# Last down projection of a two-layer decoder step: h as the stationary operand, 512 weight columns moving, the result by tokens

## The chip, the cores and the metric

The kernel runs on one core of one Trainium2 chip. The metric is the device time of one execution in microseconds (us), the median over runs. "The profiled execution" is one further execution, taken with the hardware profiler on; the views of the trace come from it alone.

## The reference, cut to what matters

There are 256 prompt tokens and 64 sample tokens (8 sequences of 8), D_MODEL is 2048, D_FF is 5632, and all is float32. The step has two layers; layer 0 mixes tokens by a convolution, layer 1 by an mLSTM cell, and each mixer is followed by a SwiGLU FFN. The change is in the FFN of layer 1, the last thing that is computed:

```python
x = x + rms_norm(mix, norm_mix_post[i])
f = swiglu_ffn(rms_norm(x, norm_ffn_pre[i]), ffn_w_gate[i], ffn_w_up[i], ffn_w_down[i])
xs[gi] = x + rms_norm(f, norm_ffn_post[i])        # y_prompt, y_sample after layer 1

def swiglu_ffn(x, w_gate, w_up, w_down):
    return _dense(jax.nn.silu(_dense(x, w_gate)) * _dense(x, w_up), w_down)

def rms_norm(x, g):                               # the mean is over the 2048 features of one token
    y = xf * lax.rsqrt(jnp.mean(xf * xf, axis=-1, keepdims=True) + RMS_EPS)
    return y * g
```

## The kernel before

**Layout.** Everything lies by features: `x`, `branch` and the rest are [128 partitions = features of a chunk, chunk, 320 tokens], with T = 320 = 256 prompt tokens and 64 sample tokens. The vectors of the norms are then columns (`vcol`), one value per partition, and a sum over the features of a token is a matmul with a matrix of ones.

**Phases, groups, units.** `plan` lays the dense products out as phases. A group is 512 output features; a unit is 256 contraction rows of weights by 512 columns (128 x 1024 floats in a slot of `raw`). The FFN of a layer is cut in two segments of D_FF: `up1a` (12 groups of 8 units), `down1a` (4 groups of 12 units), `up1b` (10 groups of 8), `down1b` (4 groups of 10). The down projection of layer 1 thus has 48 + 40 = 88 units.

**Three products for one.** Outside of `pw1`, weights and activations are split into a float32r part and the remainder (`hi` and `lo`, `hh` and `hl`), and a product is hi by hi, hi by lo, lo by hi (`unit`, L1415 to L1417). The weights are the stationary operand (128 x 128), the activations move, 320 columns at a time, and the result lands by features in a bank of PSUM. A unit of the down projection has 4 (128-feature pieces) x 2 (chunks of 128 rows) x 3 = 24 matmuls. A plain float32 matmul stands in the trace as two records, each with a weight load of its own (L1668 has 64 matmuls in the program and x128 in the trace); a float32r matmul stands there as one.

**Weights.** SP loads them unit by unit into 4 slots (`load`, L380). A load waits until `lo` of the unit four earlier was made (`lo_done`); ACT copies `raw` to `hi` when PE has used the slot's last unit (`units_used`, L561); DVE makes `lo` (L889); PE waits for `lo_done`. Both splits run AHEAD = 3 units before PE.

**Groups alternate between two halves of PSUM** (`bank_of`), four banks each. After a group of `down1a`, ACT copies the four banks to `branch` (`plain_out`); after a group of `down1b`, DVE adds them to it (`add_branch`, L912), ACT squares the sums (`squares`, L586) and DVE adds the squares up in `acc` (L904).

**The end.** After the last group: a matmul of `acc` with ones (`stat_post`, L1448), ACT's root (L567), DVE's `reciprocal` of all 320 columns (L923), then eight times branch times 1/rms (L1069) and twice x plus g times that (L1072), PE's transposes of `x` to token rows (L1744), ACT's copies to `y_rows` (L878), and SP's 12 stores (L408, L409).

```python
mm(out, hi[:, slot, kk, cols], rhs_hi[:, k, :], start=begin, stop=False, skip_group_check=True)
mm(out, hi[:, slot, kk, cols], rhs_lo[:, k, :], start=False, stop=False, skip_group_check=True)
ins = mm(out, lo[:, slot, kk, cols], rhs_hi[:, k, :], start=False, stop=end, skip_group_check=True)
```

**Other matmuls that the prediction refers to.** In the mLSTM cell, L1668 multiplies 64 stationary columns (`qw_seq[:, b, :]`) by 256 moving columns of `C0`, in plain float32, and writes alternately to partitions 0 to 63 and 64 to 127 of a bank: eight matmuls in a row. L1671 is a float32 matmul with 128 stationary columns right behind it, L1686 one of 32 rows, L1693 to L1696 are float32 matmuls on the full array.

Of the kernel before, what the change touches and what calls it, by code (L numbers as in the profile page):

```python
# [59 lines left out]
def trunk_kernel(  # L60
# [45 lines left out]
    with ctx:  # L106
# [25 lines left out]
        branch = sb("branch", [P, C, T])  # L132
        raw = sb("raw", [P, SLOTS, 2, 512])
# [7 lines left out]
        hh = sb("hh", [P, segs[0], T], F32R)  # L141
        hl = sb("hl", [P, segs[0], T], F32R)
        shared_end = at[0]
# [9 lines left out]
        root = sb("root", [P, T])  # L153
        sq = sb("sq", [P, 2, 2, T])
        acc = sb("acc", [P, T])
# [73 lines left out]
        here = [shared_at]  # L229
        y_rows = sb("y_rows", [P, 3, D], place=here)  # L230
# [19 lines left out]
        def vec(name, c, n=1):  # L250
# [39 lines left out]
        C_out, Cp_out, m_out, n_turned, n_copied, y_turned, y_copied, y_out, stored = (  # L290
            sem(n) for n in ("C_out", "Cp_out", "m_out", "n_turned", "n_copied", "y_turned", "y_copied", "y_out", "stored"))
# [30 lines left out]
        def tail_weights(j, slot):  # L322
# [5 lines left out]
            yield quads[:, :, P:2 * P], w[:, :, D + col:D + col + P]  # L328

# [40 lines left out]
        def _(sp):  # L370
# [33 lines left out]
            for k in range(C // 4):  # L404
                cols = slice(512 * k, 512 * (k + 1))
                sp.wait_ge(y_copied, 3 * (k + 1))
                for t in range(2):
                    sp.dma_start(y_prompt[0, t * P:(t + 1) * P, cols], y_rows[:, t, cols]).then_inc(y_out, 16)  # L408
                sp.dma_start(y_sample.rearrange("b t d -> (b t) d")[:, cols], y_rows[0:TS, 2, cols]).then_inc(y_out, 16)  # L409
            sp.wait_ge(y_out, 16 * 3 * (C // 4))  # L410
# [3 lines left out]
        def _(pool):  # L414
# [106 lines left out]
            pool.dma_start(n_prompt[0].rearrange("b h k -> (b h) k"), vrows[B * H:B * H + H, 0, :]).then_inc(stored, 16)  # L521
            pool.wait_ge(Cp_out, 16 * H)
# [30 lines left out]
        def _(act):  # L553
# [40 lines left out]

            def up_first_half(e):
# [3 lines left out]
            def up_second_half(e, chunk):  # L599
                act.wait_ge(up_prod, e + 1)  # L600
                s.activation(hh[:, bass.ds(chunk, 2), :], tB[:, :, :], ACT.Copy).then_inc(up_hi, 1)  # L601
# [1178 lines left out]
```

## Time and profile before

| | us |
|---|---|
| median of 3 runs | 3052.49 |
| the runs | 3052.45, 3055.36, 3052.49 |
| the profiled execution | 3051.82 |
| its span, first to last instruction | 3050.3 |
| TensorE busy | 2920.4 (96%) |
| VectorE busy | 1560.3 (51%) |
| ScalarE busy | 1074.5 (35%) |

The profiled execution took 1.52 us more than its span. Engines are PE (TensorE matmul), PEld (TensorE weight load), DVE (VectorE), ACT (ScalarE), POOL (GpSimd) and SP (SyncE, which issues the weight loads). Line numbers are those of the kernel before. Matmuls are pipelined: the length of a record is longer than the distance to the next one, so the pace of PE is read from starts.

### The profile page before, as it was taken

Reading aid. Unit: us, or ns where it says so; the run is one execution under the profiler, and the core shown is the slowest. Engines: PE = TensorE matmul, PEld = TensorE weight load, DVE = VectorE, ACT = ScalarE, POOL = GpSimd, SP = SyncE. Lnnn points to the kernel's source line nnn. Section 1 sums busy time; section 2 is a strip of 40 time slices with the busy share of each in tenths; the row PEclk is TensorE's granted clock in tenths of the full one; section 3 lists DMA queues with packets and bytes.
Section 4 is the critical chain, followed back from the end, with each engine's and each line's share of the span. In section 5 each row is a group of like instructions: output and inputs, shape, how many; then the busy total and the mean of one; then the engine's idle time right before and its main releaser. Section 6 shows DMA issues by size and latency. Waiting matters only on the chain.

```text
span 3050.3 us, 49093 instructions
## 1 busy us (share of the span) xinstructions
PE 2920.4 (96%) x18542; PEld 2765.6 (91%) x18542; DVE 1560.3 (51%) x2021; ACT 1074.5 (35%) x1267; POOL 78.6 (3%) x119
## 2 busy tenths in 40 slices
PE   8999598999999999998999999998999999999997
PEld 5777498999999999998788888998999999999997
DVE  1899946544433444445654544446544433444444
ACT  3223454433333333333333233344333333333333
POOL 2110000000000000000000000000000000000000
PEclk9999799999999999999999999999999999999999
DMA  6334143444444444444243535444444444444442
GB/s 176 125 124 124 49 147 119 150 147 151 149 148 151 150 147 151 148 150 138 76 144 116 161 108 164 136 148 127 146 151 148 148 152 148 148 151 148 148 152 90
DMA packets 374564, 423.30 MB, mean 139 GB/s; under 512 B 27034, under 2 KB 302210, under 8 KB 374114
## 3 DMA queue, kind: packets, MB, share of 16 engines
q1 hardware_dynamic: 367776, 399.61, 41.2%
q0 software_dynamic: 5744, 22.21, 2.4%
q8 instruction: 51, 0.84, 0.1%
q10 hardware_dynamic: 960, 0.38, 0.1%
q14 instruction: 33, 0.27, 0.0%
HBM read 409.22 MB, written 14.31 MB: 139 GB/s over the span
## 4 chain that ended last, share of the span: by engine, by line
PE 84%; DVE 12%; issue 2%; ACT 2%; DMA 0%; DVEq 0%; ACTq 0%; SPq 0%
PE PS L1415 26%; PE PS L1416 26%; PE PS L1417 26%; DVE branch L978 7%; PE PS L1413 1%; DVE lo L889 1%; DVE branch L1010 1%; DVE C L1346 1%; PE PS L1668 0%; PE PS L1661 0%; PE PS L1686 0%; ACT sq L679 0%; PE PS L1448 0%; PE PS L1621 0%; DVE branch L974 0%
## 5 line engine op out<-in xcount | busy, mean ns | idle before, releaser
L889 DVE TENSOR_TENSOR lo<-raw,hi 128x1024 fp32r<-128x1024 f32 x688 | 842.3, 1225 | 1140.9 <-ACT hi L561 1140.7
L1415 PE MATMUL PS<-xh,hi 128*128 128x320 f32 x4096 | 1283.9, 313 | 64.1 <-issue 34.0
L1416 PE MATMUL PS<-xl,hi 128*128 128x320 f32 x4096 | 1275.5, 311 | 0.0
L1417 PE MATMUL PS<-xh,lo 128*128 128x320 f32 x4096 | 1275.1, 311 | 0.0
L561 ACT ACTIVATE hi<-raw 128x1024 fp32r<-128x1024 f32 x688 | 724.7, 1057 | 1176.5 <-PE PS L1417 1176.5
L1415 PEld LDWEIGHTS PS<-xh,hi 128*128 128x128 f32 x4096 | 776.9, 190 | 81.4 <-issue 46.4
L1416 PEld LDWEIGHTS PS<-xl,hi 128*128 128x128 f32 x4096 | 777.3, 190 | 0.0
L1417 PEld LDWEIGHTS PS<-xh,lo 128*128 128x128 f32 x4096 | 776.3, 190 | 0.0
L1417 PE MATMUL PS<-hh,lo 128*128 128x320 f32 x1408 | 435.8, 310 | 0.0
L1416 PE MATMUL PS<-hl,hi 128*128 128x320 f32 x1408 | 435.8, 310 | 0.0
L1415 PE MATMUL PS<-hh,hi 128*128 128x320 f32 x1408 | 435.8, 310 | 0.0
L1416 PEld LDWEIGHTS PS<-hl,hi 128*128 128x128 f32 x1408 | 264.4, 188 | 0.0
L1415 PEld LDWEIGHTS PS<-hh,hi 128*128 128x128 f32 x1408 | 264.4, 188 | 0.0
L1417 PEld LDWEIGHTS PS<-hh,lo 128*128 128x128 f32 x1408 | 264.4, 188 | 0.0
L1413 PE MATMUL PS<-xg,raw 128*128 128x320 f32 x896 | 244.9, 436 | 0.0
L1413 PEld LDWEIGHTS PS<-xg,raw 128*128 128x128 f32 x896 | 171.1, 192 | 70.1 <-issue 1.4
L978 DVE SCALAR_TENSOR_TENSOR branch<-u_win,vcol,branch 128x320 f32<-128x320 f32 x420 | 206.4, 567 | 0.0
L597 ACT ACTIVATE tA<-tA 128x640 f32<-128x640 f32 x44 | 32.5, 739 | 99.2 <-DVE tA L930 99.2
L601 ACT ACTIVATE hh<-tB 128x640 f32 (+1 forms) x44 | 32.6, 741 | 90.5 <-DVE tB L937 90.5
L606 ACT ACTIVATE tB<-tB,vcol 128x320 f32<-128x320 f32 x14 | 7.1, 554 | 155.9 <-DVE tB L949 155.9
L619 ACT ACTIVATE u_win<-u_prm 128x1216 f32<-128x1216 f32 x16 | 38.8, 2427 | 17.4 <-DVE branch L978 6.5
L1322 DVE TENSOR_TENSOR tC<-root,PS 128x320 f32<-128x320 f32 x8 | 3.9, 488 | 78.9 <-ACT root L828 78.9
(277 smaller groups left out, 1310.6 us busy)
## 6 DMA issues: line engine op xcount, KB each, us to landing
raw<-in_ffn_w_gate SPq DMA_DIRECT2D x352, 256.0 KB, 2.8
raw<-in_ffn_w_up SPq DMA_DIRECT2D x352, 256.0 KB, 3.0
raw<-in_ffn_w_down SPq DMA_DIRECT2D x352, 256.0 KB, 3.3
raw<-in_conv_w_pw SPq DMA_DIRECT2D x192, 256.0 KB, 2.9
raw<-in_mlstm_w_v SPq DMA_DIRECT2D x64, 256.0 KB, 3.1
raw<-in_mlstm_w_out SPq DMA_DIRECT2D x64, 256.0 KB, 3.2
raw<-in_mlstm_w_q SPq DMA_DIRECT2D x64, 128.0 KB, 2.2
raw<-in_mlstm_w_k SPq DMA_DIRECT2D x64, 128.0 KB, 2.4
```

The source lines that it names most:

```text
L561: s.activation(hi[:, slot, :, :], raw[:, slot, :, :], ACT.Copy).then_inc(hi_done, 1)
L597: s.activation(tA[:, :, :], tA[:, :, :], ACT.Silu).then_inc(up_silu, 1)
L601: s.activation(hh[:, bass.ds(chunk, 2), :], tB[:, :, :], ACT.Copy).then_inc(up_hi, 1)
L619: s.activation(grid[:, :, 0:TP // L], past, ACT.Copy)
L889: v.tensor_tensor(lo[:, slot, :, :], raw[:, slot, :, :], hi[:, slot, :, :].bitcast(F32), ALU.subtract).then_inc(lo_done, 1)
L978: v.scalar_tensor_tensor(out=out, in0=u, scalar=w_j, in1=out, op0=ALU.mult, op1=ALU.add).then_inc(conv_step, 1)
L1010: v.scalar_tensor_tensor(out=out, in0=u, scalar=vec("w_dw", c + j * C), in1=out, op0=ALU.mult, op1=ALU.add).then_inc(tail_step, 1)
L1346: v.scalar_tensor_tensor(out=C0[:, b, :], in0=C0[:, b, :], scalar=g_state[:, b:b + 1], in1=PS[:, 5 + 2 * i, pair % 2 * DV:(pair % 2 + 1) * ...
L1413: ins = mm(out, raw[:, slot, kk, cols], xg[:, k, :], start=begin, stop=end, skip_group_check=True)
L1415: mm(out, hi[:, slot, kk, cols], rhs_hi[:, k, :], start=begin, stop=False, skip_group_check=True)
L1416: mm(out, hi[:, slot, kk, cols], rhs_lo[:, k, :], start=False, stop=False, skip_group_check=True)
L1417: ins = mm(out, lo[:, slot, kk, cols], rhs_hi[:, k, :], start=False, stop=end, skip_group_check=True)
```

## The change

For the last down projection (`down1a`, `down1b`) the operands change places. A new `unit_tok` takes the place of `unit`: the 128 tokens of a half of the prompt are the stationary operand (`hh`, `hl`), and 512 weight columns move (`hi`, `lo`), so that a unit has 2 (halves of the prompt) x 2 (chunks) x 3 = 12 float32r matmuls. The 64 sample tokens are kept in plain float32 (`h_smp`) and multiplied with the unsplit weights (`raw`), 256 columns at a time, once to partitions 0 to 63 and once to 64 to 127: 2 x 2 = 4 float32 matmuls a unit. The result lies by tokens (`b_rows`, `b_smp`). Since PE now reads `raw`, the loads of `down1a`, `up1b` and `down1b` wait for `units_used` and not for `lo_done`. POOL loads the post-norm's vector to all partitions (`g_rows`, `g_smp`) when `down1b` begins. DVE adds the group and multiplies by g at once (`tok_add`), ACT squares with a sum along the row (`tok_squares`); the norm is then one number per partition. At the end x is transposed into PSUM first and ten DVE instructions write y = y * inv + x^T, each followed by its store.

```diff
+            def unit_tok(p, g_bank, j, slot, quad, n, h_hi, h_lo):
+                pe.wait_ge(lo_done, n + (1 - UNSPLIT))
+                last_unit = j == p.units - 1
+                for t in range(3):
+                    for kk in range(2):
+                        k = 2 * j + kk
+                        begin, end = k == 0, last_unit and kk == 1
+                        if t < 2:
+                            out, rows = PS[:, g_bank + t, :], slice(t * P, (t + 1) * P)
+                            mm(out, h_hi[:, k, rows], hi[:, slot, kk, :], start=begin, stop=False, skip_group_check=True)
+                            mm(out, h_lo[:, k, rows], hi[:, slot, kk, :], start=False, stop=False, skip_group_check=True)
+                            ins = mm(out, h_hi[:, k, rows], lo[:, slot, kk, :], start=False, stop=end, skip_group_check=True)
+                        else:
+                            for r in range(2):
+                                ins = mm(PS[r * TS:(r + 1) * TS, g_bank + 2, 0:256], h_smp[:, k, :],
+                                         raw[:, slot, kk, r * 256:(r + 1) * 256], start=begin, stop=end, skip_group_check=True)
+                    if last_unit and t < 2:
+                        ins.then_inc(bank_done, 1 + t)
+                ins.then_inc(units_used, 1)
...
+                elif p.name in ("down1a", "up1b", "down1b"):
+                    sp.wait_ge(units_used, n - (SLOTS - 1))
                 else:
                     sp.wait_ge(lo_done, n - (SLOTS - 1 + UNSPLIT))
...
+            pool.wait_ge(units_used, ph["down1b"].unit0)
+            g_post = norm_ffn_post[1]
+            pool.dma_start(g_rows[:, :], g_post.rearrange("(a d) -> a d", a=1).broadcast_to([P, D])).then_inc(g_in, 16)
...
+            def tok_squares(p, local, group):
+                for t in range(3):
...
+                    s.activation(sq_wide[:, (3 * local + t) % 2, 0:n], tok_tile(b_rows, b_smp, t, local), ACT.Square,
+                                 accum_out=tok_ssq[:, t, local:local + 1]).then_inc(tok_sq, 1)
...
+                if by_token:
+                    s.activation(hh[:, bass.ds(chunk, 2), 0:TP], tB[:, :, 0:TP], ACT.Copy)
+                    s.activation(h_smp[:, bass.ds(chunk, 2), :], tB[:, :, TP:T], ACT.Copy).then_inc(up_hi, 1)
...
+            def tok_add(p, local, group):
+                b = bank_of(group)
+                for t in range(3):
+                    wait_bank(dve, p, local, (0, 2, 3)[t])
+                    n = 512 if t < 2 else 256
+                    v.tensor_tensor(tok_tile(b_rows, b_smp, t, local), tok_tile(b_rows, b_smp, t, local), PS[:, b + t, 0:n],
+                                    ALU.add).then_inc(tok_out if t < 2 else banks_read, 1)
...
+                    v.tensor_tensor(tok_tile(y_rows, y_smp, t, local), tok_tile(b_rows, b_smp, t, local), g_t,
+                                    ALU.mult).then_inc(tok_scaled, 1)
...
-            squares(db, db.groups - 1, db.group0 + db.groups - 1)
-            stat(9, (PS[:, BANKS * ((db.group0 + db.groups - 1) % 2), 0:T], root[:, :]))
...
+            s.activation(tok_root[:, 4:5], ones[:, 0:1], ACT.Sqrt)
+            tok_squares(db, db.groups - 1, db.group0 + db.groups - 1)
+            act.wait_ge(tok_summed, 1)
+            s.activation(tok_root[:, 0:2], tok_sum[:, 0:2], ACT.Sqrt, bias=eps[:, 0:1], scale=1.0 / D)
+            act.wait_ge(tok_folded, 1)
+            s.activation(tok_root[:, 2:3], PS[:, last_bank + 2, 511:512], ACT.Sqrt, bias=eps[:, 0:1], scale=1.0 / D).then_inc(tok_rooted, 1)
...
-            add_branch(db, db.groups - 1, db.group0 + db.groups - 1)
-            inverse(9, rp)
-            for j in range(C // 2):
-                prep_front_part("end", j)
+            tok_add(db, db.groups - 1, db.group0 + db.groups - 1)
+            dve.wait_ge(tok_sq, 3 * db.groups)
+            v.tensor_reduce(tok_sum[:, 0:3], tok_ssq[:, :, :], mybir.AxisListType.X, ALU.add).then_inc(tok_summed, 1)
+            dve.wait_ge(tok_rooted, 1)
+            v.reciprocal(tok_inv[:, 0:3], tok_root[:, 0:3]).then_inc(tok_inverse, 1)
...
+            for i, (t, k) in enumerate(Y_CHUNKS):
+                dve.wait_ge(y_turned, i + 1)
+                v.scalar_tensor_tensor(out=y_chunk(t, k), in0=y_chunk(t, k), scalar=tok_inv[:, t:t + 1],
+                                       in1=PS[:, Y_BANKS[i % 8], :], op0=ALU.mult, op1=ALU.add).then_inc(y_ready, 1)
```

On PE, the last unit and the end, before (`acc`, `ones`: the sum over features; `ident`: transposes of x):

```order
L1417 MATMUL PS<-hh,lo 128x320
L1606 REGISTER_ALU
L1606 COMPARE_AND_BRANCH
L1448 MATMUL PS<-acc,ones 128x320 [waits br_acc]
L1744 MATMUL PS<-ident,x 128x128 [waits prep_front]
L1744 MATMUL PS<-ident,x 128x128 x7
L1744 MATMUL PS<-ident,x 64x128 x4
```

On PE at the same place now, with the changed kernel's line numbers (`fold` sums the two halves of the sample's row sums; L1874 and L1878 transpose x):

```order
L1526 MATMUL PS<-hi,hh 128x512
L1527 MATMUL PS<-hi,hl 128x512
L1528 MATMUL PS<-lo,hh 128x512
L1531 MATMUL PS<-raw,h_smp 64x256 x4
L1719 REGISTER_ALU
L1719 COMPARE_AND_BRANCH
L1874 MATMUL PS<-ident,x 128x128 [waits banks_read]
L1874 MATMUL PS<-ident,x 128x128 x15
L1878 MATMUL PS<-ident,x 64x128 x8
L1865 MATMUL PS<-tok_sum,fold 64x1 [waits tok_summed,banks_read]
```

The four 64-column matmuls now end every unit, and 24 matmuls of the transposition go ahead of the wait for the row sums.

On DVE after the last split of weights, before:

```order
L912 TENSOR_TENSOR branch<-branch,PS 128x320 x4
L904 TENSOR_TENSOR acc<-acc,sq 128x320 x4
L923 RECIPROCAL rp<-root 128x320
L1069 TENSOR_TENSOR branch<-branch,rp 128x640 x2
L1072 SCALAR_TENSOR_TENSOR x<-branch,vcol,x 128x320 x2
L1069 TENSOR_TENSOR branch<-branch,rp 128x640
```

And now:

```order
L990 TENSOR_TENSOR b_rows<-b_rows,PS 128x512 x2
L990 TENSOR_TENSOR b_smp<-b_smp,PS 128x256
L1000 TENSOR_TENSOR y_rows<-b_rows,g_rows 128x512 x2
L1000 TENSOR_TENSOR y_smp<-b_smp,g_smp 128x256
L1478 TENSOR_REDUCE tok_sum<-tok_ssq 128x3
L1480 RECIPROCAL tok_inv<-tok_root 128x3
L1485 SCALAR_TENSOR_TENSOR y_rows<-y_rows,tok_inv,PS 128x512 x4
```

The multiplication by g moved ahead of the norm, the sum of squares left DVE, and the reciprocal shrank from 320 columns to 3.

## Rows read from the trace of the kernel before

**Rows 1.** The page: busy time and the clock granted, in 40 slices
```profile
span 3050.3 us, 49093 instructions
...
PE 2920.4 (96%) x18542; PEld 2765.6 (91%) x18542; DVE 1560.3 (51%) x2021; ACT 1074.5 (35%) x1267; POOL 78.6 (3%) x119
...
PEclk9999799999999999999999999999999999999999
...
PE 84%; DVE 12%; issue 2%; ACT 2%; DMA 0%; DVEq 0%; ACTq 0%; SPq 0%
```
**Rows 2.** Stretches of down1a, down1b and the end: window, length, busy (records)
```profile
2433.00:2602.00 169.00, 169.00 (x1154) 169.00 (x1153) 61.20 (x52) 55.55 (x53) 0.00 (x0) 1.00 0.45 150
2883.60:3024.40 140.80, 140.80 (x962) 140.72 (x960) 59.95 (x69) 46.58 (x53) 0.00 (x0) 1.00 0.38 127
3024.40:3050.30 25.90, 9.13 (x52) 7.07 (x50) 17.89 (x30) 9.31 (x16) 0.00 (x0) 0.80 0.30 101
```
**Rows 3.** Timeline of PE in down1b: start, length
```profile
2999.78 0.31 PE L1415 MATMUL PS<-hh,hi 128*128 128x320 f32 x1
...
3000.95 0.31 PE L1417 MATMUL PS<-hh,lo 128*128 128x320 f32 x1
```
**Rows 4.** Timeline of PE where the granted clock was half
```profile
1448.47 0.47 PE L1417 MATMUL PS<-xh,lo 128*128 128x320 f32 x1
1448.74 0.47 PE L1415 MATMUL PS<-xh,hi 128*128 128x320 f32 x1
1449.01 0.47 PE L1416 MATMUL PS<-xl,hi 128*128 128x320 f32 x1
```
**Rows 5.** Timeline of PE, float32 on the full array
```profile
1577.25 0.31 PE L1417 MATMUL PS<-xh,lo 128*128 128x320 f32 x1
1577.40 0.70 PE L1693 MATMUL PS<-sq,ones 128*128 128x320 f32 x2
1577.93 0.70 PE L1694 MATMUL PS<-sq,ones 128*128 128x320 f32 x2
1578.47 0.60 PE L1695 MATMUL PS<-v_tok,kw 128*128 128x256 f32 x2
1578.90 0.59 PE L1696 MATMUL PS<-v_tok,kw 128*128 128x256 f32 x2
```
**Rows 6.** Timeline of PE around L1668, and the length of one of its records
```profile
1516.63 0.31 PE L1417 MATMUL PS<-xh,lo 128*128 128x320 f32 x1
1516.87 1.95 PE L1668 MATMUL PS<-C,qw_seq 128*64 128x256 f32 x16
1518.75 0.80 PE L1671 MATMUL PS<-rows_h,ones 8*128 8x320 f32 x2
...
L1668 PE MATMUL PS<-C,qw_seq x128: 378/379/432, 1516.9 to 1851.3; 128*64 128x256 f32 x128
```
**Rows 7.** Timeline of PE, back from a 32-row form to the full array
```profile
1581.34 0.42 PE L1415 MATMUL PS<-xh,hi 128*128 128x320 f32 x1
1581.59 0.31 PE L1416 MATMUL PS<-xl,hi 128*128 128x320 f32 x1
1581.74 0.31 PE L1417 MATMUL PS<-xh,lo 128*128 128x320 f32 x1
```
**Rows 8.** Timeline of all engines at the end
```profile
3024.27 0.31 PE L1417 MATMUL PS<-hh,lo 128*128 128x320 f32 x1
...
3024.62 0.49 DVE L912 TENSOR_TENSOR branch<-branch,PS 128x320 f32<-128x320 f32 x1 [0.39 <-PE PS L1417]
...
3047.49 0.47 SPq L409 DMA_DIRECT2D out_y_sample<-y_rows  x1
```
**Rows 9.** Groups by line and form from 3024.4 us to the end
```profile
L1072 DVE SCALAR_TENSOR_TENSOR x<-branch,vcol,x 128x320 f32<-128x320 f32 x16 | 8.0, 544 | 0.0
L1069 DVE TENSOR_TENSOR branch<-branch,rp 128x640 f32<-128x640 f32 x8 | 6.5, 818 | 0.0
...
L923 DVE RECIPROCAL rp<-root 128x320 f32<-128x320 f32 x1 | 2.2, 2152 | 1.5 <-ACT root L567 1.5
```
**Rows 10.** Weights from 2433 us on: time to landing, and the splits of a unit
```profile
DMA to landing us min/median/max: 2.7/3.3/4.1
...
L889 DVE TENSOR_TENSOR lo<-raw,hi 128x1024 fp32r<-128x1024 f32 x146 | 179.0, 1226 | 287.1 <-ACT hi L561 287.1
...
L561 ACT ACTIVATE hi<-raw 128x1024 fp32r<-128x1024 f32 x146 | 154.4, 1058 | 278.7 <-PE PS L1417 278.7
```

More of the change, by code:

```diff
@@ L328, in tail_weights, with tok_tile, y_chunk @@
             yield quads[:, :, P:2 * P], w[:, :, D + col:D + col + P]
+        Y_CHUNKS = []
+        for q in range(D // 1024):
+            Y_CHUNKS += [(t, k) for k in (2 * q, 2 * q + 1) for t in range(2)] + [(2, q)]
+        last_bank = bank_of(ph["down1b"].group0 + ph["down1b"].groups - 1)
+        Y_BANKS = [BANKS - last_bank + m for m in range(BANKS)] + [last_bank + 3, last_bank, last_bank + 1, last_bank + 2]
+        def tok_tile(rows, smp, t, k):
+            return rows[:, t, bass.ds(k * 512, 512)] if t < 2 else smp[:, k, :]
+        def y_chunk(t, k):
+            return y_rows[:, t, 512 * k:512 * (k + 1)] if t < 2 else y_smp[:, 2 * k:2 * k + 2, :].rearrange("p a n -> p (a n)")
         def acc_count(p, g, m):
@@ L1206, in ffn @@
                     last = up_window(up.groups)
-                    if down is db:
+                    if down is db and l == 0:
                         last[3] = [lambda: clear_acc()]
@@ L1210, in ffn @@
                     for w in range(1, down.groups):
-                        window(down, w, split, {} if down is da else {0: [lambda: add_branch(db, w - 1, db.group0 + w - 1)]})
+                        window(down, w, split, {} if down is da else {0: [lambda: (tok_add if l else add_branch)(db, w - 1, db.group0 + w - 1)]})
             dve.wait_ge(u_out, 16 * (B + 1))
@@ L1599, in wait_h, with down @@
                     pe.wait_ge(h_ready, up_first[up.name] + j + 1)
-                group(da, 0, {j: [lambda j=j: wait_h(a, j)] for j in range(da.units)})
-                with pe.Fori(1, da.groups) as g:
-                    group(da, g)
+                def down(up, p):
+                    first_bank = bank_of(p.group0)
+                    with pe.Fori(0, p.groups // 2) as it:
+                        group(p, it * 2, {j: [lambda j=j: wait_h(up, j)] for j in range(p.units)}, rep=0, bank=first_bank)
+                        group(p, it * 2 + 1, rep=1, bank=BANKS - first_bank)
+                if l:
+                    down(a, da)
+                else:
+                    group(da, 0, {j: [lambda j=j: wait_h(a, j)] for j in range(da.units)})
+                    with pe.Fori(1, da.groups) as g:
+                        group(da, g)
                 phase(b_)
-                with pe.Fori(0, db.groups // 2) as it:
-                    group(db, it * 2, {j: [lambda j=j: wait_h(b_, j)] for j in range(db.units)}, rep=0)
-                    group(db, it * 2 + 1, rep=1)
+                down(b_, db)
             ffn(0, 0)
```

132 lines of the change are left out of this document (94 added, 38 removed).

## The prediction

> **What bounds the kernel now.** I read the page first: TensorE is busy 96% of the span, and the chain that ended last is 84% TensorE and 12% VectorE [rows 1]. So two questions decide: how long PE needs for the 88 units of the last down projection, and how long the stretch after PE's last product is.
>
> The table by stretch answers the first for the kernel before. In down1a and down1b PE is busy for the whole 169.0 and 140.8 us, at the full granted clock (1.00, that is 2.4 GHz), with 1154 and 962 records [rows 2]. PE waits for nothing there: its pace alone sets the time. The timeline gives the pace: eight steps from 2999.78 to 3000.95, 0.1465 us each [rows 3]; 169.0 / 1154 gives the same. A unit of 24 matmuls takes 24 x 0.1465 = **3.52 us**, and 88 units 309.5 us. ACT and DVE are busy a third of that stretch, and the DMA engines 0.38 to 0.45 of it [rows 2].
>
> The last record of PE's products starts at 3024.27 and the span ends at 3050.3: an **end of 26.0 us** [rows 1, 8]. In it DVE is busy 17.9 of 25.9 us [rows 2]; it is DVE's work that is passed through one after another there.
>
> **The float32r part of a unit.** 24 matmuls of 320 columns become 12 of 512. No row shows a 512-column float32r matmul, so its pace S is bounded. At full clock 320 columns would stream in 320 / 2.4 = 133.3 ns, and 146.5 are seen: 13.2 ns over. At half the clock (0.50, 1.2 GHz) the same records start 0.267 apart [rows 4], which is 320 / 1.2 with nothing over. Lowest: plain float32 passes its columns twice a record; L1695 and L1696, 256 columns, hence 512 column passes, start 0.43 apart for two records, 0.216 each [rows 5]. Highest: the excess grows with the columns, 146.5 x 512 / 320 = 0.2345. Between them: 13 ns a matmul whatever its length, 213.3 + 13.3 = 0.2267. I take **0.2267**. The float32 rows show that there the excess is one per record: 0.269 for 640 column passes (1577.40 to 1577.93 is 0.53 for two), 2 to 3 ns over, and 0.216 for 512, also 2 to 3 over [rows 5]. The float32r row is nearer to that than to a rate. Against the lowest value speaks that the stretch from the last float32r matmul to L1693 is 0.15, not 0.136 [rows 5]: the matmul itself takes the longer time, not the fetch of the next float32r weights. So 12 x 0.2267 = 2.72 us, against 3.52 for all 320 tokens before.
>
> The Trainium skill (TensorE: Matmul & The Clock Gate, "Back-to-back issue gap") gives N / 2.4 + 2.5 ns for an isolated matmul. For 320 columns that is 135.8 ns, which the float32r rows here don't follow, though the float32 rows do; for 512 it is 215.8, my lowest value.
>
> **The sample part of a unit.** 4 float32 matmuls, 8 records of 256 columns, on 64 stationary columns that alternate between the halves of the array. L1668 is the same form: 16 records in 1.95 us [rows 6]. If they ran one by one as L1695 does, it would be 15 x 0.216 + 0.38 = 3.6 us. They run two at a time: 8 pairs, 0.216 a pair. So 4 pairs, 4 x 0.216 = 0.86 us a unit.
>
> **The change of array form.** Twice a unit PE goes from 128 stationary columns to 64 and back. The rows around L1668 price it. From the last float32r record to the first pair 0.24 where 0.147 is usual: +0.09. In the group, the last pair starts 1.95 - 0.38 = 1.57 after the first, and seven steps are 1.51: +0.06 (I use 0.05, rounding being 0.01 a row). From the last pair, 1518.44, to L1671 at 1518.75 is 0.31 where 0.216 is usual: +0.09 [rows 6]. The first float32r record back on the full array is followed after 0.25 instead of 0.147: +0.10 [rows 7]. Together **0.33 to 0.34 us a unit**. The lower bound is nothing, were the next weights fetched under the running matmul; but there is no row in which a change cost nothing, and float32r to float32 without a change of form costs none (0.15) [rows 5].
>
> The Trainium skill (TensorEngine Tiling (Array Packing), "Performance Considerations") recommends for 64 or fewer moving columns just this: swap stationary and streaming operand, and tile by columns twofold. The rows agree with the twofold pace. The same page ("Key Properties") says that changing the tiling mode drains the engine, without a price; the 0.34 us are this case's price, and they speak against the change.
>
> **Sum over the units.** 2.72 + 0.86 + 0.34 = 3.92 us instead of 3.52: +0.40 a unit, x 88 = **+35.5 us**. In columns: 7680 before; now 12 x 512 + 4 pairs x 512 = 8192. The change saves columns only if the 12 saved excesses of 13 ns (0.16 us) weigh more than 512 further columns (0.21 us) and the change of form (0.34). They don't.
>
> **Work beside it, at nothing.** ACT's and DVE's split of a unit takes 1.06 and 1.23 us of 3.9 [rows 10]. The adds and multiplications of tok_add come once in ten units, about 3.3 us on DVE (below); the copy of the sample's h is one ACT instruction more a group; clear_acc goes. The loads' wait moves: SP may now refill a slot only when PE has used it. Then issue, landing (4.1 at most), ACT 1.06, DVE 1.23 [rows 10], some 7.3 us with two issues of 0.4 (as L409 [rows 8]), against the three units, 11.8 us, that PE still has in stock (10.6 us in up1b). Behind the later landing stand on ACT the silu and the squares, on DVE lo and the additions; all have a group (28 us or more) before PE waits for them. If this cover were gone, each microsecond of lateness beyond would be paid by PE. POOL's three transfers of g come once, 1.5 MB beside weights that take 0.38 of the DMA engines, 38 us before their first reader: nothing, at most 3 us if they delay weights.
>
> **The end.** DVE instructions of 320 columns run 0.49 to 0.54, of 640 0.82 [rows 8, 9], so 512 columns take about 0.69, and 0.66 in a row; 256 take 0.42. From the start of PE's last pair: that pair ends and DVE begins the last addition +0.42; it ends +0.84; three multiplications by g to +2.6; row sums +2.8. PE meanwhile makes 16 transposes and 8 small matmuls from +0.3 to +3.2, then the fold of the sample's sums, +3.6; ACT's root +4.0; DVE's reciprocal of 3 columns +4.2 (it was 2.15 for 320 [rows 9]); ten instructions of 0.68 to +11.1; then two stores, the last issued at about +11.6. In the kernel before the last issue stands 2.8 us ahead of the span's end [rows 1, 8]. End: **14.4 us instead of 26.0, -11.6**. What goes is DVE's second pass (L1069, 6.5 us), the long reciprocal, the addition of squares, and ACT's copies behind the last x. Bounds: -9.5 if the roots wait for each other longer, -13 if PE is done earlier than I say.
>
> **Sum.** 3051.8 (profiled execution) + 35.5 - 11.6 = 3075.7, say **3076 us**. The median shown, 3052.5, is 0.7 above that execution, less than 0.2% (6 us), about what a measurement of this kernel can tell from no change.
>
> **The rivals.**
> - *The excess grows with the columns*, S = 0.2345: unit 2.81 + 0.86 + 0.34 = 4.01, +43.5 - 11.6 gives 3084. For it: one length only is seen. Chance 22%.
> - *S is 0.216*: unit 2.59 + 0.86 + 0.34 = 3.79, +24 - 11.6 gives 3064. For it: the pace of float32 per pass. Against it: the 0.15 before L1693. Chance 15%. The rule of TensorE: Matmul & The Clock Gate in the Trainium skill, above, comes to the same.
> - *Faster: the change of form is hidden.* If the weights of the other form are fetched under the running 512-column matmuls and nothing drains, the unit is 2.72 + 0.86 = 3.58, +5.5 - 11.6 gives 3046; with S = 0.216 3.46, -5.6 - 11.6 gives 3034.6. The point from which it decides: a unit under 3.52 + 11.6 / 88 = 3.65 us. Against it: rows 6 and 7 show the price on entry and on return. Chance 9%.
> - *The halves don't overlap.* 8 records at 0.216 one after the other are 1.73: unit 4.79, +112 - 11.6 gives 3152. Against it: L1668. Chance 2%.
> - *Late weights.* PE waits for lo once landings pass about 8 us; twice the longest seen. A microsecond a unit would give some 3160. Chance 2%.
>
> **How the numbers follow.** The forecast has 50%, with 3 us to both sides for the end and the price of the change of form. The range takes in S = 0.216 below and the growing excess above, with 2 to 3 us of the end each: 3061 to 3087; left out are the hidden change, the overlap and the late weights, 13%, and the edges. Faster by over 0.2% is the hidden change in both forms, 0.07 of its 0.09. Within 0.2% (3046.4 to 3058.6) is a part of it, and a half-hidden change, 0.08. Slower 0.85.
>
> **What would show it.** In the profile of the changed kernel: starts of L1526 to L1528 0.227 apart (0.216, 0.2345 for the rivals); L1531 as four pairs 0.216 apart; a gap of some 0.09 before and after them and 0.33 after the first float32r matmul; starts of units 3.92 apart; PE still busy throughout and at full clock, with ACT's hi waiting for weights, not PE for lo; 14 to 15 us from the last L1531 to the end. Wrong is the prediction if units start under 3.65 apart, or if PE waits for lo_done, or if the granted clock falls in these stretches, which no row with PE steadily at work shows.

## The result and the profile after

The changed kernel takes **3083.43 us** (median; 3078.04 to 3084.80), the kernel before, timed beside it, 3052.47 (3045.44 to 3055.36). The ratio is 1.0106, with a 95% interval of 1.0085 to 1.0126: slower by 31 us. The forecast was 3076, with 3061 to 3087 as its range. The profiled execution took 3084.80 (before 3051.82), so 33.0 us are to be found.

The page of the changed kernel, its busy times, the clock granted and the chain that ended last:

```profile
span 3083.3 us, 48416 instructions
...
PE 2961.0 (96%) x18208; PEld 2689.1 (87%) x18208; DVE 1545.9 (50%) x1999; ACT 1070.3 (35%) x1291; POOL 80.3 (3%) x122
...
PEclk9999799999999999999999999999999999999999
...
PE 84%; DVE 11%; issue 2%; ACT 2%; DMA 0%; DVEq 0%; SPq 0%; ACTq 0%
```

Beside [rows 1] PE has 334 records fewer and is busy 40.6 us longer; the clock is the same slice by slice, and DVE's part of the chain falls from 12 to 11%. The same three stretches as in [rows 2] (window, length, busy and records of PE, PEld, DVE, ACT, POOL, granted clock, share of the DMA engines, GB/s):

```profile
2435.30:2627.20 191.90, 191.90 (x963) 127.64 (x961) 61.73 (x52) 56.12 (x58) 0.00 (x0) 1.00 0.40 132
2908.90:3068.90 160.00, 160.00 (x803) 106.43 (x802) 59.91 (x63) 49.02 (x64) 1.83 (x3) 1.00 0.40 132
3068.90:3083.30 14.40, 6.01 (x68) 5.21 (x67) 8.85 (x16) 1.51 (x6) 0.00 (x0) 0.82 0.54 182
```

PE is busy for the whole of both down stretches and at the full clock, as before. Counted from their first record of PE to their last, down1a went from 168.8 to 191.5 us and down1b from 140.65 to 159.5; the end behind the last product went from 26.0 to 14.85 us. That is +22.7 + 18.9 - 11.2 = +30.4, and 0.3 in up1b between them. The other 2.3 us lie ahead of the change: down1a begins at 2435.3 instead of 2433.1, in code that the change doesn't touch. In the kernels below it begins anywhere from 2426.9 to 2434.0. Much of that goes with the granted clock: in the rounds of the experiments the kernel before took 3052.4 to 3055.4 us in its eight runs with a mean granted clock of 0.981 over the span, and 3045.0 to 3048.0 in its nine with 0.983 or 0.984. Two further executions of it took over 8500 us and are left out as disturbed.

One unit in the timeline of PE (start, length, line; from the first row of one unit to the first of the next):

```profile
2952.75 0.50 PE L1526 MATMUL PS<-hi,hh 128*128 128x512 f32 x1
2953.09 0.40 PE L1527 MATMUL PS<-hi,hl 128*128 128x512 f32 x1
...
2955.41 0.39 PE L1528 MATMUL PS<-lo,hh 128*128 128x512 f32 x1
2955.73 1.08 PE L1531 MATMUL PS<-raw,h_smp 128*64 128x256 f32 x8
2956.75 0.50 PE L1526 MATMUL PS<-hi,hh 128*128 128x512 f32 x1
```

From 2952.75 to 2956.75 is a unit: **4.000 us** from start to start, the same to the ns in both stretches, but for the first unit of each (3.86 and 3.85), which has no sample part in front of it. The forecast said 3.92, and it was 3.52. The start times of the trace in ns give the distances below, the same to a few ns in all units that follow another:

```
float32r 1st to 2nd           341
2nd to 12th               240 235 233 236 224 231 236 228 233 230
last float32r to first pair   318
starts within the four pairs  7 260 7 209 7 209 7
last record to next unit      309
```

The ten distances in the second line are the surprise: nine of them lie over the 0.2267 of the forecast, and they sum to 2.326 us instead of 2.267.

The waits of the changed kernel from 2435 to 3070 us (engine, line, what it waited for; total us, times, longest), and from the DMA view of that stretch the time to landing of the weights:

```profile
DVE lo L957 <- ACT hi L606: 378.0, 164, 5.8
ACT hi L606 <- DMA raw<-in_ffn_w_down: 221.8, 78, 4.7
...
PEld PS L1526 <- DVE lo L957: 2.3, 6, 0.4
```
```profile
DMA to landing us min/median/max: 2.7/3.1/8.6
```

ACT's wait has moved from PE, by which a slot comes free, to the transfer itself, as the refill by PE's use of the slot makes it. The last line is PE's weight load, not its matmuls: 0.4 us stands ahead of L1526 in 80 other units too, put down there to "issue", and the units start 4.000 apart throughout. So PE lost nothing to late weights.

The end, in the timeline of all engines:

```profile
3067.73 1.08 PE L1531 MATMUL PS<-raw,h_smp 128*64 128x256 f32 x8
...
3068.87 0.42 DVE L990 TENSOR_TENSOR b_smp<-b_smp,PS 128x256 f32<-128x256 f32 x1 [0.34 <-PE PS L1531]
...
3071.85 0.26 ACT L946 ACTIVATE tok_root<-PS,eps 128x1 f32<-128x1 f32 x1 [0.62 <-PE PS L1865]
3072.14 0.17 DVE L1480 RECIPROCAL tok_inv<-tok_root 128x3 f32<-128x3 f32 x1 [1.24 <-ACT tok_root L946]
3072.35 2.72 DVE L1485 SCALAR_TENSOR_TENSOR y_rows<-y_rows,tok_inv,PS 128x512 f32<-128x512 f32 x4
...
3078.29 0.74 DVE L1485 SCALAR_TENSOR_TENSOR y_smp<-y_smp,tok_inv,PS 128x512 f32<-128x512 f32 x1
3079.34 1.56 SPq L447 DMA_DIRECT2D out_y_sample<-y_smp  x2
```

From the start of the last pair, 3068.43, the last addition begins after 0.44 us (forecast 0.42), the reciprocal is done after 3.9 (4.2) and the last of the ten blocks after 10.6 (11.1). The last store is issued at +11.8 (11.6), and the span ends 3.0 behind it (2.8), so that the half microsecond is lost again. The second pass, L1069's 6.5 us, and the reciprocal of 2.15 us [rows 9] are gone.

### The profile page after: what moved, and what is told of

The parts are those of the page before. It is cut to its first block, busy times and chain, and to the rows that moved or that the text cites. A ratio compares the mean times of both kernels' runs of the same rounds, so it can differ in the third digit from the quotient of the medians.

```text
span 3083.3 us, 48416 instructions
## 1 busy us (share of the span) xinstructions
PE 2961.0 (96%) x18208; PEld 2689.1 (87%) x18208; DVE 1545.9 (50%) x1999; ACT 1070.3 (35%) x1291; POOL 80.3 (3%) x122
## 4 chain that ended last, share of the span: by engine, by line
PE 84%; DVE 11%; issue 2%; ACT 2%; DMA 0%; DVEq 0%; SPq 0%; ACTq 0%
PE PS L1509 22%; PE PS L1511 22%; PE PS L1510 22%; DVE branch L1065 7%; PE PS L1526 3%; PE PS L1531 3%; PE PS L1527 3%; PE PS L1528 3%; PE PS L1507 1%; DVE lo L957 1%; DVE branch L1097 1%; DVE C L1433 1%; PE PS L1790 0%; PE PS L1783 0%; PE PS L1808 0%
## 5 line engine op out<-in xcount | busy, mean ns | idle before, releaser
L1509 PE MATMUL PS<-hh,hi 128*128 128x320 f32 x704 | 217.5, 309 | 0.0
L1510 PE MATMUL PS<-hl,hi 128*128 128x320 f32 x704 | 217.5, 309 | 0.0
L1511 PE MATMUL PS<-hh,lo 128*128 128x320 f32 x704 | 217.5, 309 | 0.0
L1526 PE MATMUL PS<-hi,hh 128*128 128x512 f32 x352 | 148.4, 422 | 0.0
L1527 PE MATMUL PS<-hi,hl 128*128 128x512 f32 x352 | 139.8, 397 | 0.0
L1528 PE MATMUL PS<-lo,hh 128*128 128x512 f32 x352 | 137.3, 390 | 0.0
L1509 PEld LDWEIGHTS PS<-hh,hi 128*128 128x128 f32 x704 | 132.1, 188 | 0.0
L1510 PEld LDWEIGHTS PS<-hl,hi 128*128 128x128 f32 x704 | 132.1, 188 | 0.0
L1511 PEld LDWEIGHTS PS<-hh,lo 128*128 128x128 f32 x704 | 132.1, 188 | 0.0
L1526 PEld LDWEIGHTS PS<-hi,hh 128*128 128x128 f32 x352 | 65.9, 187 | 45.9 <-issue 30.8
L1531 PE MATMUL PS<-raw,h_smp 128*64 128x256 f32 x704 | 95.4, 392 | 0.0
```

The lines of the kernel that those rows point to most:

```text
L1526: mm(out, h_hi[:, k, rows], hi[:, slot, kk, :], start=begin, stop=False, skip_group_check=True)
L1527: mm(out, h_lo[:, k, rows], hi[:, slot, kk, :], start=False, stop=False, skip_group_check=True)
L1528: ins = mm(out, h_hi[:, k, rows], lo[:, slot, kk, :], start=False, stop=end, skip_group_check=True)
L1531: ins = mm(PS[r * TS:(r + 1) * TS, g_bank + 2, 0:256], h_smp[:, k, :], raw[:, slot, kk, r * 256:(r + 1) * 256], start=begin, stop=end, ski ...
```

## The experiments

Two questions. Where do the 0.08 us a unit come from that the forecast lacked: does the excess of a float32r matmul grow with its columns (the forecast's first rival), or is something slower behind a float32 part? And is the 0.34 us for the change of form what it was taken for? Behind them stands a third, whether the gain at the end can be had without the loss in the body.

**e1: the sample part left out of most units.**

```diff
-                for t in range(3):
+                for t in range(3 if j == 0 or last_unit else 2):
```

> The sample tokens' part is left out of 72 of the 88 units of the down projection (it stays in the first and the last unit of each group), so their down projection is incomplete. In the changed kernel a unit takes exactly 4.00 us and its float32r matmuls of 512 columns start 0.2324 apart on average (with the two changes of form taken off), where 0.2267 was forecast. Theory 1, the excess over 512 / 2.4 belongs to the length: the matmuls stay at 0.232, a unit without the sample part takes 2.79 us, the profiled execution 72 x 1.21 = 87 us less than 3085: 2998. Theory 2, it is an after-effect of the change of array form: without one they start 0.227 apart, the unit takes 2.72 and the execution 2993. Either says that the sample part with its changes of form is 1.21 (1.28) us of the 4.00. If PE then waits for weights, the gap stands before the first matmul of a unit and not between the others.

Measured: 2988.31 us. The stretches first to last are 140.4 and 121.2 us. PE in the middle of a run of units without a sample part:

```profile
2461.16 0.39 PE L1527 MATMUL PS<-hi,hl 128*128 128x512 f32 x1
2461.39 0.39 PE L1528 MATMUL PS<-lo,hh 128*128 128x512 f32 x1
2461.61 0.39 PE L1526 MATMUL PS<-hi,hh 128*128 128x512 f32 x1
```

The starts are 227 and 226 ns apart, here and along the run: 0.2267, the value chosen from [rows 3] and [rows 5]. Behind the few sample parts that are left, the ten distances are again 240 235 233 236 224 231 236 228 233 230, and the eleventh is 227. So it isn't the 512 columns alone that make a matmul slow, but its place. Without them a unit is 2.72 us instead of 4.00. In down1a the 40 units without a sample part took 51.2 us off, 1.28 each. In down1b the 32 took 38.3 instead of 41.0, mostly since PE, now faster, stood still for 2.0 us. The 96.5 us to the profile of the changed kernel are these two and 7.0 ahead of down1a.

**e2: the pace by length.** As e1, and the float32r matmuls shortened, 256 columns in down1a and 384 in down1b.

```diff
+                            n_cols = 512 if j == 0 or last_unit else 256 if p.name == "down1a" else 384
-                            out, rows = PS[:, g_bank + t, :], slice(t * P, (t + 1) * P)
+                            out, rows = PS[:, g_bank + t, 0:n_cols], slice(t * P, (t + 1) * P)
...
-                            mm(out, h_hi[:, k, rows], hi[:, slot, kk, :], start=begin, stop=False, skip_group_check=True)
+                            mm(out, h_hi[:, k, rows], hi[:, slot, kk, 0:n_cols], start=begin, stop=False, skip_group_check=True)
```

> As the run without the sample part, but in those 72 units only the first 256 columns (down1a) or 384 columns (down1b) of the weights are multiplied, so columns are left out too; read are only the distances between matmuls inside a unit at full clock, not the time. Known: 0.1465 for 320 columns, 0.2324 for 512. Theory 1, the excess grows with the columns: a straight line through the two gives 0.118 for 256 and 0.175 for 384. Theory 2, a fixed 13 ns a matmul: 0.120 and 0.173. Theory 3, strictly proportional to 320: 0.117 and 0.176. The line and the fixed excess are told apart by 384 within 2 ns and by 512 in the other run. The units will wait for weights, since 12 x 0.118 = 1.4 us is less than a landing allows.

Measured: 2961.29 us; at the one length and at the other:

```profile
2459.90 0.28 PE L1527 MATMUL PS<-hi,hh 128*128 128x256 f32 x1
2460.02 0.28 PE L1528 MATMUL PS<-hi,hl 128*128 128x256 f32 x1
...
2900.00 0.33 PE L1527 MATMUL PS<-hi,hh 128*128 128x384 f32 x1
2900.17 0.33 PE L1528 MATMUL PS<-hi,hl 128*128 128x384 f32 x1
```

Distances of 120, 173 to 174 and (first and last units) 227 ns; with the 146.5 of [rows 3] that makes four lengths:

| columns | ns between starts | columns / 2.4 | over |
|---|---|---|---|
| 256 | 120 | 106.7 | 13.3 |
| 320 | 146.5 | 133.3 | 13.2 |
| 384 | 173.3 | 160.0 | 13.3 |
| 512 | 226.7 | 213.3 | 13.4 |

The excess is one per matmul whatever its length. The first rival of the forecast is out, although its 3084 is next to the measured time.

**e3: twice the changes of form.** The two loops are exchanged, so that a unit's sample part falls into two of two pairs each. The work is the same.

```diff
-                for t in range(3):
-                    for kk in range(2):
+                for kk in range(2):
+                    for t in range(3):
...
-                    if last_unit and t < 2:
-                        ins.then_inc(bank_done, 1 + t)
+                        if end and t < 2:
+                            ins.then_inc(bank_done, 1 + t)
```

> The same matmuls with the sample part after each of the two chunks of a unit instead of once at its end: two changes to the 64-column form and two back in a unit instead of one each, nothing else changed. If a change of form costs what the rows show (0.10 on entry, 0.05 in the first pair, 0.09 and 0.10 on return, 0.34 together), a unit takes 4.34 instead of 4.00 and the execution is 88 x 0.34 = 30 us longer: 3115. If the cost is not one of the change but of the two kinds of work, 3085 stays.

Measured: 3114.91 us, on the expected value. One half of a unit:

```profile
2952.22 0.65 PE L1531 MATMUL PS<-raw,h_smp 128*64 128x256 f32 x4
2952.80 0.50 PE L1526 MATMUL PS<-hi,hh 128*128 128x512 f32 x1
2953.14 0.39 PE L1527 MATMUL PS<-hi,hl 128*128 128x512 f32 x1
...
2954.07 0.40 PE L1528 MATMUL PS<-lo,hh 128*128 128x512 f32 x1
2954.40 0.65 PE L1531 MATMUL PS<-raw,h_smp 128*64 128x256 f32 x4
2954.98 0.50 PE L1526 MATMUL PS<-hi,hh 128*128 128x512 f32 x1
```

Half a unit is 2.18 us, the unit 4.36 instead of 4.00. The first distance of 0.34, the 0.33 ahead of the pairs, and the 0.58 from the first pair to the return stand twice in it. The slow distances sum to what they did, 60 ns over in the unit. Both stretches together grew by 31.7 us (208.86 + 173.96 - 191.55 - 159.54), 0.36 for each of the 88 round trips added. By the ns of the changed kernel a round trip costs 91 (entry) + 51 (in the pairs) + 100 (exit) + 114 (first distance after) = 356 ns, the same. [Rows 6, 7] had said 0.34.

**e6: the sample part without the change of form.** Its stationary side is 128 prompt tokens, its moving side 512 columns, in plain float32 on the full array.

```diff
-                            for r in range(2):
-                                ins = mm(PS[r * TS:(r + 1) * TS, g_bank + 2, 0:256], h_smp[:, k, :],
-                                         raw[:, slot, kk, r * 256:(r + 1) * 256], start=begin, stop=end, skip_group_check=True)
+                            ins = mm(PS[:, g_bank + 2, :], h_hi[:, k, P:TP].bitcast(F32), raw[:, slot, kk, :],
+                                     start=begin, stop=end, skip_group_check=True)
```

> In the changed kernel the sample part's stationary operand is replaced by 128 tokens of the prompt, so that the full array is used, with 512 moving columns in plain float32 (4 records a unit in place of 8): no change of form, but the same change between float32r and float32; the sample's output is not computed. If the 0.34 us and the slower matmuls behind them belong to the change of array form, the float32r matmuls start 0.227 apart throughout, the first float32 record follows at the usual distance, and a unit takes 12 x 0.2267 + 4 x 0.429 = 4.44 us: 88 x 0.44 = 38 us more than the changed kernel, 3122. If they belong to the change of number format, a unit takes 4.44 + 0.4 = 4.85 and the execution 3158.

Measured: 3120.30 us. Into the float32 part and out of it:

```profile
2949.74 0.39 PE L1528 MATMUL PS<-lo,hh 128*128 128x512 f32 x1
2949.97 1.88 PE L1530 MATMUL PS<-raw,hh 128*128 128x512 f32 x4
2951.29 0.79 PE L1526 MATMUL PS<-hi,hh 128*128 128x512 f32 x1
2951.92 0.40 PE L1527 MATMUL PS<-hi,hl 128*128 128x512 f32 x1
```

Entry takes 0.23, the usual distance. Out of it, the first float32r record starts early (28 ns behind the last float32 record) and the second 0.63 later; the two together are 660 ns, where one float32 record (429) and one float32r matmul (227) make 656. So without a change of form neither entry nor return has a price, and the 0.36 belong to the change between the full array and the two halves used in turn. Whether the 64 columns or the taking of turns makes it, no run separates. But the next ten distances are 235 234 236 224 231 235 229 232 231 227, 47 ns over ten undisturbed ones. So the slow stretch behind doesn't need the change of form. That the plain float32 makes it isn't shown either: the first unit of down1b stands straight behind up1b's float32r matmuls of 320 columns, 0.1465 apart, and begins in the changed kernel, in e1, e4, e6 and e7 with the distances 231 236 228 233 230, within 1 ns, 25 ns over in five, before it goes on at 227. The 88 units took 42.8 us more than in the changed kernel (4.487 a unit, not 4.44), and 7.5 less were spent ahead of them; that the total came within 2 us of the expected 3122 is these two together.

**e4: the sample part once in two units.** Half the changes of form, the same products; a slot comes free a unit later.

```diff
-                for t in range(3):
-                    for kk in range(2):
-                        k = 2 * j + kk
+                for t in range(3 if j % 2 else 2):
+                    for k in range(2 * j, 2 * j + 2) if t < 2 else range(2 * j - 2, 2 * j + 2):
+                        kk = k % 2
...
-                ins.then_inc(units_used, 1)
+                if j % 2:
+                    ins.then_inc(units_used, 2)
```

> The sample part of two units is computed together behind the second one: half as many changes of form, the whole result computed. The price is that a slot of raw weights is free up to a unit later. By the price of a change: 44 x 0.34 = 15 us less, 3070, still slower than before (3052). Rival: the slots come free too late (issue, landing, two splits together 6.4 to 7.3 us against two units, 7.7 us): PE waits for lo, and the gain is lost or turns into a loss, to be seen as idle time of PE before L1526.

Measured: median **3063.36 us** (3060.88 to 3068.18), ratio to the kernel before 1.0048, interval 1.0032 to 1.0064: still slower than before, and 7 us under what was expected. Around a sample part of two units:

```profile
2455.10 1.95 PE L1532 MATMUL PS<-raw,h_smp 128*64 128x256 f32 x16
2456.97 0.50 PE L1526 MATMUL PS<-hi,hh 128*128 128x512 f32 x1
...
2458.24 0.39 PE L1528 MATMUL PS<-lo,hh 128*128 128x512 f32 x1
2458.47 0.39 PE L1526 MATMUL PS<-hi,hh 128*128 128x512 f32 x1
2458.69 0.39 PE L1527 MATMUL PS<-hi,hl 128*128 128x512 f32 x1
```

The slow stretch is not only met half as often, it is also shorter behind the longer float32 part: five distances of 236 to 226, then 227, some 21 ns over instead of 59. In down1a that accounts for all: 24 round trips fewer are 24 x 0.356 = 8.5 us, the slow stretches 48 x 0.059 - 24 x 0.021 = 2.3, and the stretch went from 191.5 to 180.6, by 10.9. In down1b the same sum gives 9.1, but only 3.5 came (159.5 to 156.0). There PE now does stand still, its busy time being 4.2 us short of the window:

```profile
2426.80:2612.00 185.20, 185.20 (x991) 135.87 (x990) 61.62 (x52) 55.84 (x58) 0.00 (x0) 1.00 0.41 138
2894.00:3045.90 151.90, 147.67 (x782) 105.66 (x782) 57.53 (x60) 48.06 (x64) 0.00 (x0) 1.00 0.39 132
```

Here a slot is held a unit longer, and the cover that made the later refill free in the changed kernel is used up: its price, nothing there, is 5.0 us here, in five waits for lo of 0.4 to 1.9 us. Four of them stand 10 us into a group. The longest is in the first group, where a landing took 8.9 us just after POOL's g transfers were issued; in the three other groups the ACT copy to `hi` comes straight behind the squares of the group before, which stand ahead of it on that engine. The body thus shrank by 14.5 us, as the forecast for this run had it, but by two terms that it lacked and that nearly cancel. The rest of the distance to 3083 lies ahead of the change: in this profile down1a begins at 2426.9, 8.5 us earlier than in the profile of the changed kernel, on instructions that are the same. Most of it goes with the granted clock. From 1400 to 1650 us, in the changed kernel and here:

```profile
1400.00:1650.00 250.00, 224.89 (x1365) 197.95 (x1364) 142.18 (x243) 88.52 (x121) 10.52 (x19) 0.94 0.40 119
1400.00:1650.00 250.00, 224.87 (x1392) 199.28 (x1391) 144.37 (x245) 88.04 (x120) 10.49 (x19) 0.96 0.41 123
```

With a granted clock of 0.96 and not 0.94, PE got 27 more records done in the same time, some 4 us of work at 0.1465. Over the span the mean is 0.985 here and 0.982 there. Why it differs from one execution to the next, no run tells. Run against run at the same mean, e4 takes 3068.2 where the changed kernel takes 3082.9 to 3084.8 (0.982), and 3060.9 and 3063.4 where it takes 3078.0 (0.984): 15 to 17 us less, which is the forecast's 15.

**e7: the shorter matmuls of e2, with the sample part in every unit.** Does the slow stretch shrink with the length of the matmuls?

```diff
-                for t in range(3 if j == 0 or last_unit else 2):
+                for t in range(3):
```

(the rest as e2)

> As e2_lengths (256 moving columns in down1a, 384 in down1b, but for the first and last unit of a group; columns are left out), but with the sample part in every unit. In the changed kernel the ten float32r matmuls behind the second of a unit take together 0.06 us more than at their undisturbed pace, also where the sample part used the full array. Read is that sum at 256 and 384 columns, against 0.120 and 0.1733 undisturbed. Theory 1, a constant disturbance a record behind a float32 part: 0.06 again at both lengths. Theory 2, only records of more than some length show it (behind the 32-row matmuls of the kernel before, at 320 columns, it was under 0.01): near 0 at 256, 0.06 or less at 384. The change of form itself: 0.10, 0.05, 0.09 and 0.10 us at every length.

Measured: 3003.13 us. A unit at 384 columns:

```profile
2873.41 0.44 PE L1527 MATMUL PS<-hi,hh 128*128 128x384 f32 x1
2873.69 0.34 PE L1528 MATMUL PS<-hi,hl 128*128 128x384 f32 x1
2873.86 0.34 PE L1529 MATMUL PS<-lo,hh 128*128 128x384 f32 x1
...
2875.42 0.34 PE L1529 MATMUL PS<-lo,hh 128*128 128x384 f32 x1
2875.69 1.08 PE L1532 MATMUL PS<-raw,h_smp 128*64 128x256 f32 x8
2876.71 0.44 PE L1527 MATMUL PS<-hi,hh 128*128 128x384 f32 x1
```

From the second matmul of a unit on, the pace is 0.174 at once, 3 ns over ten undisturbed distances; at 256 columns the same sum is 12 ns under them. The first distance stays about 0.1 over the pace at both lengths, the entry +0.09, and the 309 ns to the next unit are the same. So the price of the change of form hardly depends on the length: 342, 354 and 356 ns at 256, 384 and 512 columns. The slow stretch was seen at 512 columns alone. Of the 14 units of this run that have 512 and stand behind a sample part, the six whose unit before has 512 too show 59 ns, and the eight behind a unit of 256 or 384 columns 20. So the matmuls ahead of the sample part have a share in it as well. Why it needs the length, and what starts and shortens it, isn't settled: no run looked at lengths between 384 and 512.

**h1: the kernel before with only the end by rows.** The body keeps the old form. ACT makes branch x g beside the last down projection, the last group's additions and squares are woven together, three small products give the row sums, PE turns x and branch x g in one ring of seven banks, ACT moves the turned x, and one DVE instruction a block makes y, which is stored block by block.

```diff
+                    if p.name == "down1b" and local < p.groups - 1:
+                        s.activation(bg[:, chunk, :], branch[:, chunk, :], ACT.Copy, scale=vec("ffn_post1", chunk)).then_inc(bg_ready, 1)
...
-            for j in range(C // 2):
-                prep_front_part("end", j)
...
+                        ins = mm(PS[0:nn, last_bank + 3, tt:tt + 1], acc[:, tt * P:tt * P + nn], ones[:, 0:1],
+                                 start=tt == 0, stop=True, skip_group_check=True)
...
+                v.scalar_tensor_tensor(out=y_rows[0:n, t, cols], in0=PS[0:n, place_of["b", i], :], scalar=tok_inv[0:n, t:t + 1],
+                                       in1=y_rows[0:n, t, cols], op0=ALU.mult, op1=ALU.add).then_inc(y_ready, 1)
```

> The kernel before with its own body (weights stationary, 3.52 us a unit) and only the end of the change, adapted: row sums of squares by three matmuls with one moving column, branch times g and x both transposed to token rows, y = branch^T x inv + x^T in twelve DVE instructions of 512 columns, each with its store. The whole result is computed. By the end measured in the changed kernel (14.9 instead of 26.0 us) and 48 more transposes of 0.109 on PE, which then is the slowest there: 96 x 0.109 = 10.5 + 0.9 for the sums and the start, then one DVE instruction and the store, about 15.5 us: 10.5 us less than the kernel before, 3042. Rival: the end's gain needs the layout by tokens, that is the new body; then the transposes and the copies of x by ACT (12 x 0.6 = 7 us) eat it and the time is within 3 us of 3052.

Measured over five rounds: median **3037.59 us** (3036.15 to 3039.75) against 3049.81 for the kernel before in the same rounds (3045.03 to 3055.35); ratio 0.9961, interval 0.9948 to 0.9975. It beats both kernels. Its last down stretch and its end, by stretch, and its end in the timeline:

```profile
2878.50:3019.30 140.80, 140.80 (x962) 140.80 (x961) 60.30 (x71) 52.78 (x68) 0.00 (x0) 1.00 0.38 127
3019.30:3035.70 16.40, 11.55 (x104) 11.08 (x102) 11.71 (x22) 7.78 (x16) 0.00 (x0) 0.97 0.49 161
```
```profile
3021.18 0.78 PE L1802 MATMUL PS<-ones,acc 128*128 128x1 f32 x6
...
3022.44 0.17 DVE L1440 RECIPROCAL tok_inv<-tok_root 128x2 f32<-128x2 f32 x1 [0.22 <-ACT tok_root L902]
...
3022.70 9.60 DVE L1448 SCALAR_TENSOR_TENSOR y_rows<-PS,tok_inv,y_rows 128x512 f32<-128x512 f32 x12
```

The stretch of down1b is 140.8 us with 962 records, as in [rows 2], and the end is 16.5 us instead of 26.0. It is 1.6 longer than in the changed kernel: the reciprocal comes as early (3.3 us behind the start of the last product, there 3.7), but twelve blocks take 9.6 us of DVE where ten took 6.7; the last store follows closer. The end's 9.5 us are most of the 12.2 between the medians. The rest goes with the granted clock: it was 0.984 to 0.986 in the runs of h1 and 0.981 to 0.984 in those of the kernel before, and at 0.984 alone the two kernels' runs lie 7.7 us apart on average (3038.6, 3046.3).

## Why the prediction came out

**What bounds the kernel: right.** PE was busy throughout both down stretches, before and after, at the full clock. The time is PE's pace times 88 units and the end.

**The float32r part of a unit: the pace right, its constancy wrong.** "12 x 0.2267 = 2.72 us" is the term that was mis-sized. The pace of an undisturbed 512-column matmul is 0.2267 (e1), with the fixed excess of 13.3 ns that was argued from four rows (e2). But behind each sample part the next ten matmuls sum to 59 ns more. That is 88 x 0.059 = 5.2 us; another 88 x 0.016 = 1.4 us is the round trip of form, 0.356 and not 0.34 (return 0.114 for 0.10, exit 0.10 for 0.09). Together the unit is 4.00 and not 3.92, which makes 6.6 us over the 88; 6.4 were seen. The rows that could have warned were few: what follows a plain float32 part in the kernel before are 320-column matmuls, and at 384 columns and fewer the stretch is not slow (e7).

The rival with the growing excess gave 3084 and the run 3083.4. It is wrong all the same: e2 refutes it. A total that fits does not show the mechanism. And the range held by its help: 3087, the upper bound, is that rival's 3084 and 3 us, while the forecast's own mechanism with its 3 us to both sides ends at 3079. That is luck. The rule of the Trainium skill (TensorE: Matmul & The Clock Gate, "Back-to-back issue gap") for an isolated matmul, N / 2.4 + 2.5 ns, which would have given 0.2158 and an estimate of 3064, doesn't hold for these float32r matmuls at any of the four lengths in the table at e2.

**The sample part: right.** Four pairs at 0.216 (the rows: 209 + 7 ns). The halves overlap.

**The change of form: right.** 0.34 us a unit was forecast from the rows around L1668, 0.356 is measured; e3 doubled it and gave 0.36 for each more, e6 took it away and entry and return cost nothing. The hidden change, the rival on the other side, would have needed a unit under 3.65; none was. (Its sum with S = 0.216 has a slip: 3.46 instead of 3.516 us, 88 times, is -5 and not -5.6. Nothing hangs on it.) The Trainium skill (TensorEngine Tiling (Array Packing), "Key Properties") says that a change of tiling mode drains the engine. The costs that e3 and e6 measured agree with that, and are its price here; the drain itself no row shows.

**The work beside it: at nothing, right; the landings wrong.** One landing took 8.6 us while POOL's g transfers ran, twice the forecast's 4.1 and over the 8 us from which it saw PE waiting; the others took 4.6 at most. "If PE waits for lo_done" was one of its signs of being wrong, and the view of waits does name lo six times, but the units kept their 4.000 us. e4 shows how near the edge that is: holding a slot for a unit more cost 5 us.

**The end: right.** 14.85 us for 14.4, at no step more than 0.5 off.

**Against the profiled execution.** Body +41.9 where +35.5 was forecast, end -11.2 where -11.6 was, and 2.3 us ahead of the change that no step of it explains: +33.0. The three miss to the same side, so nothing cancelled.

Why the exchange loses is now in measured terms. Per unit, the prompt tokens would take 24 x 0.120 = 2.88 us with 256 tokens moving (an estimate, by e2's pace), and take 2.72 with 512 weight columns moving: 0.16 saved. The 64 sample tokens took 24 x 0.0267 = 0.64 us as 64 more moving columns, and now take 0.86 for the pairs, 0.36 for the change of form and 0.06 for the slow stretch behind: 1.28, so 0.64 lost. The difference is the unit's 0.48. The gain at the end, 11.2 us, comes from another part of the change, and h1 has 9.5 of it without the loss.

## What to carry to other kernels

Where PE is busy all the time, cost a change of layout by the ns from start to start of each form, and count every passage between forms and types beside the columns: here the saving on the matmuls was 0.16 us a unit, and the passages alone cost 0.42. If a change joins a gain at one place with a loss at another, try whether the gain stands alone; h1 was the better kernel. And shift the parts that need another form or type into as few places as the buffers allow, as e4 did, watching what they hold.

## What the runs showed of the hardware

- A float32r matmul at the full clock takes its columns / 2.4 ns and 13.3 ns more, at 256, 320, 384 and 512 columns; at half the clock there was nothing over at 320 [rows 4].
- Behind a plain float32 part, five to ten float32r matmuls of 512 columns are slower: by 59 ns in sum behind 8 records on array halves, 47 behind 4 records on the full array, 21 behind 16 records on halves, 20 behind 8 where shorter float32r matmuls stood before them (e7). Behind float32r matmuls of 320 columns, with no float32 part between, it is 25 ns. At 384 columns it is 3 ns. This was not expected, and its cause is open.
- Going from 128 stationary columns to 64 and back costs 0.356 us, of which 0.09 lie ahead of the first pair, 0.05 behind it, 0.10 behind the last pair and 0.11 in the first matmul after; none of it where only the type changes (e6). With 256 and 384 moving columns around it is 0.342 and 0.354 (e7).
- The same kernel (the one before) took some 7 us less in executions with a higher mean granted clock: 3052.4 to 3055.4 us at 0.981, 3045.0 to 3048.0 at 0.983 and 0.984.
- The sample part in float32r on the two halves, which would spare the second pass of each record, was not tried on the chip; whether the slow stretch would go with it stays open.
